# Last feed-forward down projection of a two-block model: seven block products instead of eight, in two parts of the contracted channels

## The reference, cut to what matters

```python
D_MODEL, D_FF = 1024, 2816
# block 2, after its mixers; x is (1, 1024 tokens, 1024 channels)
h = modulate(x, g_2, shift_2, scale_2)
u = depthwise_conv(h @ w_up_2, ffn_conv_w_2) + ffn_conv_b_2
gate, val = split(u, 2, axis=-1)
x = x + gate_2 * ((silu(gate) * val) @ w_down_2)      # 2816 -> 1024, the product of this case
out = rms_norm(x, final_norm_g_2)
```

## Time and profile before

| what | value |
|---|---|
| device time, median of 3 runs | 5803.57 us (5803.05 to 5805.03) |
| profiled execution: span of its instructions | 5800.0 us |
| mean granted TensorE clock | 0.923 of full speed |
| TensorE busy (matmuls) | 4973.6 us, 86% |
| VectorE, ScalarE, GpSimd busy | 1681.9, 1308.9, 551.3 us |
| last down projection, matmuls of L438 | 704, 305.1 us busy |
| the same, TensorE idle ahead of it | 16.7 us |

### The profile page before, as it was taken

One profiled execution on the slowest core, in us unless ns is written; L12 is line 12 of the kernel. 1 busy time (PEld: TensorE's weight loads), 2 busy tenths in 40 slices (PEclk: granted clock), 3 DMA queues, 4 the chain that ended last, 5 costly groups with the idle time before them and its releaser, 6 DMA issues. The chain is left out here.

```text
span 5800.0 us, 68474 instructions
## 1 busy us (share of the span) xinstructions
PE 4973.6 (86%) x27313; PEld 2658.2 (46%) x27313; DVE 1681.9 (29%) x3062; ACT 1308.9 (23%) x2074; POOL 551.3 (10%) x443
## 2 busy tenths in 40 slices
PE   6688888887989778999989778787888886999898
PEld 2254564532644533444434326556656632444344
DVE  5433243203611611111100145444515612111101
ACT  2222122102410611222200113222214402222100
POOL 0020121100010010000000013222200002000000
PEclk9898888898999889999999889888989998999999
DMA  3501101110021021111033111111010001111111
GB/s 76 81 18 33 31 7 34 34 44 11 1 74 47 33 87 33 36 40 36 29 113 107 42 39 38 43 43 40 7 39 1 1 29 33 40 36 40 31 40 52
DMA packets 301970, 232.18 MB, mean 40 GB/s; under 512 B 30771, under 2 KB 266982, under 8 KB 301670
## 3 DMA queue, kind: packets, MB, share of 16 engines
q1 hardware_dynamic: 301706, 228.40, 14.0%
HBM read 203.69 MB, written 24.67 MB: 39 GB/s over the span
## 5 line engine op out<-in xcount | busy, mean ns | idle before, releaser
L624 PE MATMUL psum<-ffn_in,up_slots 128*128 128x512 f32 x2816 | 1212.9, 594 | 54.3 <-DMA up_slots<-in_w_up_dram 35.8
L624 PEld LDWEIGHTS psum<-ffn_in,up_slots 128*128 128x128 f32 x2816 | 536.4, 191 | 730.8 <-issue 730.8
L661 DVE SCALAR_TENSOR_TENSOR conv<-u,conv_cols_a,conv 128x1024 f32<-128x1024 f32 x88 | 113.0, 1284 | 983.3 <-ACT conv L643 983.3
L438 PE MATMUL psum<-hidden,w_slots 128*128 128x512 f32 x704 | 305.1, 596 | 16.7 <-DMA w_slots<-in_w_down_dram 16.7
L2248 PE MATMUL psum<-hidden,w_slots 128*128 128x512 f32 x704 | 306.3, 596 | 9.6 <-DMA w_slots<-in_ffn_w_down_dram 9.6
L640 ACT ACTIVATE u<-psum 128x512 f32<-128x512 f32 x176 | 105.1, 597 | 892.8 <-PE psum L624 892.8
L2774 PE MATMUL psum<-h,w_slots 128*128 128x512 f32 (+1 forms) x576 | 219.7, 542 | 38.3 <-issue 36.1
L675 POOL TENSOR_TENSOR hidden<-conv 128x1024 f32 x44 | 103.1, 2343 | 1317.5 <-DVE conv L665 1317.5
L438 PEld LDWEIGHTS psum<-hidden,w_slots 128*128 128x128 f32 x704 | 134.7, 191 | 187.1 <-issue 169.6
L2248 PEld LDWEIGHTS psum<-hidden,w_slots 128*128 128x128 f32 x704 | 133.9, 191 | 176.7 <-issue 166.8
L1532 PE MATMUL psum<-x,w_slots 128*128 128x512 f32 x384 | 175.4, 620 | 34.1 <-issue 23.8
(11 more groups left out here) (552 smaller groups left out, 7504.7 us busy)
## 6 DMA issues: line engine op xcount, KB each, us to landing
mod_slots<-in_w_mod_dram SPq DMA_DIRECT2D x12, 2048.0 KB, 8.1
up_slots<-in_ffn_w_up_dram SPq DMA_DIRECT2D x44, 512.0 KB, 3.8
up_slots<-in_w_up_dram SPq DMA_DIRECT2D x44, 512.0 KB, 3.9
w_slots<-in_w_in_dram SPq DMA_DIRECT2D x38, 512.0 KB, 5.0
w_slots<-in_ffn_w_down_dram SPq DMA_DIRECT2D x8, 1408.0 KB, 12.4
w_slots<-in_w_down_dram SPq DMA_DIRECT2D x8, 1408.0 KB, 7.0
rows_in<-in_x_dram SPq DMA_DIRECT2D x16, 512.0 KB, 3.6
gate_w<-in_w_in_dram SPq DMA_DIRECT2D x16, 512.0 KB, 6.0
```

The costliest lines, as they stand in the source:

```text
L438: last = nc.tensor.matmul(T.ps[2 * s + j][:, :], slots[:, s, k, :], rhs(k)[:, j * HALF:(j + 1) * HALF], start=(k == 0), stop=(k == kt - 1))
L624: last = nc.tensor.matmul(T.ps[b][:, :], slots[:, q, k, :], h[:, k, j * HALF:(j + 1) * HALF], start=(k == 0), stop=(k == KD - 1))
L661: nc.vector.scalar_tensor_tensor(out=conv[:, q, :], in0=u[:, q, first:first + S], scalar=conv_w[first][:, bass.ds(col, 1)], in1=conv[:, q, :],
```

## The change

`block_product` takes the place of `add_product` in this one call. Output channels, contracted channels and tokens are each cut in two, and the four quarter results are made from seven products of quarter size instead of eight. A is the weight matrix: a11 and a12 are the weights of output block n (n = 0 to 3) from the first and second 11 blocks of contracted channels; a21 and a22 are those of output block n + 4. B is `hidden`: b11 and b12 are the first 11 channel blocks for the early and late 512 tokens, b21 and b22 the last 11.

The weight sums s1 = a21 + a22, s2 = s1 - a11, s3 = a11 - a21, s4 = a12 - s2 are made on GpSimd for each output pair. The activation sums t1 = b12 - b11, t2 = b22 - t1, t3 = b22 - b12, t4 = b21 - t2 are made on VectorE. t3 overwrites b12 in `hidden`, and s3 overwrites a21. The products are p1 = a11 b11, a12 b21, p6 = s2 t2, p7 = s3 t3, p5 = s1 t1, a22 t4 and s4 b22. With u2 = p1 + p6 and u3 = u2 + p7 the quarters are p1 + a12 b21, u2 + p5 + s4 b22, u3 + a22 t4 and u3 + p5.

The 11 blocks are handled in two parts, of 6 and then 5 blocks, so there are eight steps: (part 0, n = 0 to 3), then (part 1, n = 0 to 3). One step has seven products of 6 (or 5) matmuls of 512 columns. Step i uses banks 4 (i mod 2) to 4 (i mod 2) + 3. The turn between the parts, where VectorE remakes the t's for part 1, is in step 3 (`turn`). Four DMAs (384 KB each in part 0, 320 KB in part 1) load a step's weights.

```diff
--- before.py
+++ after.py
@@ -452,6 +452,161 @@
                                 nc.vector.scalar_tensor_tensor(
                                     out=xs, in0=T.ps[2 * s + j][:, :], scalar=gate[:, bass.ds(i * 2 + s, 1)],
                                     in1=xs, op0=ALU.mult, op1=ALU.add).then_inc(kept[2 * s + j], 1)
+def block_product(nc, T, w, rhs, x, gate):
+    KH = KF // 2
+    EARLY, LATE = slice(0, HALF), slice(HALF, S)
+    first_n = (KH + 1) // 2
+    spans = ((0, first_n), (first_n, KH))
+    pairs = KD // 2
+    steps = [(part, n) for part in range(2) for n in range(pairs)]
...
+    with sbuf(nc, "act_sums", [P, 3, first_n, HALF]) as act_sums, sbuf(nc, "down_slots", [P, 2, 2, 2, first_n, P]) as slots, \
+            sbuf(nc, "down_sums", [P, 2, 3, first_n, P]) as sums, sbuf(nc, "partial", [P, 2, HALF]) as partial, \
+            sbuf(nc, "partial_3", [P, HALF]) as partial_3:
...
+            weights = (weights_even, weights_odd)
+            width = lambda part: spans[part][1] - spans[part][0]
+            def weight(i, block_half, channel_half):
+                return slots[:, i % 2, block_half, channel_half, 0:width(steps[i][0]), :]
+            a11, a12, a21, a22 = (lambda i: weight(i, 0, 0)), (lambda i: weight(i, 0, 1)), (lambda i: weight(i, 1, 0)), (lambda i: weight(i, 1, 1))
+            s1, s2, s4 = (lambda i: sums[:, i % 2, 0, 0:width(steps[i][0]), :]), (lambda i: sums[:, i % 2, 1, 0:width(steps[i][0]), :]), \
+                (lambda i: sums[:, i % 2, 2, 0:width(steps[i][0]), :])
+            s3 = a21
+            b11 = lambda part: rhs[:, spans[part][0]:spans[part][1], EARLY]
+            b12 = lambda part: rhs[:, spans[part][0]:spans[part][1], LATE]
+            b21 = lambda part: rhs[:, KH + spans[part][0]:KH + spans[part][1], EARLY]
+            b22 = lambda part: rhs[:, KH + spans[part][0]:KH + spans[part][1], LATE]
+            t1, t2, t4 = (lambda part: act_sums[:, 0, 0:width(part), :]), (lambda part: act_sums[:, 1, 0:width(part), :]), \
+                (lambda part: act_sums[:, 2, 0:width(part), :])
+            t3 = b12
+            @block.sync
+            def _(sp):
+                for i, (part, n) in enumerate(steps):
+                    if i >= 2:
+                        sp.wait_ge(c12_made, i - 1)
+                    for bh in range(2):
+                        cols = weight_cols(w, KF, (n + bh * pairs) * P)
+                        for ch in range(2):
+                            sp.dma_start(weight(i, bh, ch), cols[:, ch * KH + spans[part][0]:ch * KH + spans[part][1], :]
+                                         ).then_inc(weights[i % 2], 16)
+            @block.gpsimd
+            def _(pool):
+                for i in range(len(steps)):
+                    pool.wait_ge(weights[i % 2], 64 * (i // 2 + 1))
+                    if i >= 2:
+                        pool.wait_ge(c12_made, i - 1)
+                    nc.gpsimd.tensor_tensor(s1(i), a21(i), a22(i), ALU.add).then_inc(sums_made, 1)
+                    pool.wait_ge(sums_made, 4 * i + 1)
+                    nc.gpsimd.tensor_tensor(s2(i), s1(i), a11(i), ALU.subtract).then_inc(sums_made, 1)
+                    nc.gpsimd.tensor_tensor(s3(i), a11(i), a21(i), ALU.subtract).then_inc(sums_made, 1)
+                    pool.wait_ge(sums_made, 4 * i + 2)
+                    nc.gpsimd.tensor_tensor(s4(i), a12(i), s2(i), ALU.subtract).then_inc(sums_made, 1)
+            @block.tensor
+            def _(pe):
+                def product(bank, lhs, moving, first=True):
+                    kt = lhs.shape[1]
+                    for k in range(kt):
+                        last = nc.tensor.matmul(T.ps[bank][:, :], lhs[:, k, :], moving[:, k, :], start=(first and k == 0), stop=(k == kt - 1),
+                                                skip_group_check=not first)
+                    return last
+                for i, (part, n) in enumerate(steps):
+                    ba, bb, bc, bd = (4 * (i % 2) + j for j in range(4))
+                    pe.wait_ge(weights[i % 2], 64 * (i // 2 + 1))
+                    if i >= 2:
+                        pe.wait_ge(c11_added, i - 1)
+                    product(ba, a11(i), b11(part)).then_inc(p1_made, 1)
+                    if n == 0:
+                        pe.wait_ge(acts_made, 4 * part + 4)
+                    pe.wait_ge(sums_made, 4 * i + 4)
+                    if i >= 2:
+                        pe.wait_ge(u2_made, i - 1)
+                    product(bb, s2(i), t2(part)).then_inc(p6_made, 1)
+                    pe.wait_ge(p1_kept, i + 1)
+                    product(ba, a12(i), b21(part), False).then_inc(c11_made, 1)
+                    if i >= 2:
+                        pe.wait_ge(c21_added, i - 1)
+                    product(bc, s3(i), t3(part)).then_inc(p7_made, 1)
+                    if i >= 2:
+                        pe.wait_ge(c12_added, i - 1)
+                    product(bd, s1(i), t1(part)).then_inc(p5_made, 1)
+                    pe.wait_ge(u3_made, i + 1)
+                    product(bc, a22(i), t4(part), False).then_inc(c21_made, 1)
+                    pe.wait_ge(c22_added, i + 1)
+                    product(bd, s4(i), b22(part), False).then_inc(c12_made, 1)
+            @block.scalar
+            def _(act):
+                for i in range(len(steps)):
+                    act.wait_ge(p1_made, i + 1)
+                    if i >= 2:
+                        act.wait_ge(u_added, 3 * (i - 1))
+                    nc.scalar.activation(partial[:, i % 2, :], T.ps[4 * (i % 2)][:, :], ACT.Copy).then_inc(p1_kept, 1)
+            @block.vector
+            def _(dve):
+                def add_to(out_block, tokens, src, added):
+                    xs = x[:, out_block, tokens]
+                    if gate is None:
+                        nc.vector.tensor_tensor(xs, xs, src, ALU.add).then_inc(added, 1)
+                    else:
+                        nc.vector.scalar_tensor_tensor(out=xs, in0=src, scalar=gate[:, out_block:out_block + 1], in1=xs,
+                                                       op0=ALU.mult, op1=ALU.add).then_inc(added, 1)
+                nc.vector.tensor_tensor(t1(0), b12(0), b11(0), ALU.subtract).then_inc(acts_made, 1)
+                dve.wait_ge(acts_made, 1)
+                nc.vector.tensor_tensor(t2(0), b22(0), t1(0), ALU.subtract).then_inc(acts_made, 1)
+                nc.vector.tensor_tensor(t3(0), b22(0), b12(0), ALU.subtract).then_inc(acts_made, 1)
+                dve.wait_ge(acts_made, 2)
+                nc.vector.tensor_tensor(t4(0), b21(0), t2(0), ALU.subtract).then_inc(acts_made, 1)
+                for i, (part, n) in enumerate(steps):
+                    ba, bb, bc, bd = (T.ps[4 * (i % 2) + j][:, :] for j in range(4))
+                    turn = part == 0 and n == pairs - 1
+                    u2 = partial[:, i % 2, :]
+                    dve.wait_ge(p6_made, i + 1)
+                    dve.wait_ge(p1_kept, i + 1)
+                    nc.vector.tensor_tensor(u2, u2, bb, ALU.add).then_inc(u2_made, 1)
+                    dve.wait_ge(c11_made, i + 1)
+                    add_to(n, EARLY, ba, c11_added)
+                    dve.wait_ge(p7_made, i + 1)
+                    dve.wait_ge(u2_made, i + 1)
+                    if i >= 1:
+                        dve.wait_ge(u_added, 3 * i)
+                    nc.vector.tensor_tensor(partial_3[:, :], u2, bc, ALU.add).then_inc(u3_made, 1)
+                    dve.wait_ge(p5_made, i + 1)
+                    add_to(n + pairs, LATE, bd, c22_added)
+                    if turn:
+                        nc.vector.tensor_tensor(t1(1), b12(1), b11(1), ALU.subtract).then_inc(acts_made, 1)
+                        dve.wait_ge(acts_made, 5)
+                        nc.vector.tensor_tensor(t2(1), b22(1), t1(1), ALU.subtract).then_inc(acts_made, 1)
+                        nc.vector.tensor_tensor(t3(1), b22(1), b12(1), ALU.subtract).then_inc(acts_made, 1)
+                    dve.wait_ge(u3_made, i + 1)
+                    dve.wait_ge(c22_added, i + 1)
+                    add_to(n + pairs, LATE, partial_3[:, :], u_added)
+                    dve.wait_ge(c21_made, i + 1)
+                    add_to(n + pairs, EARLY, bc, c21_added)
+                    if turn:
+                        dve.wait_ge(acts_made, 6)
+                        nc.vector.tensor_tensor(t4(1), b21(1), t2(1), ALU.subtract).then_inc(acts_made, 1)
+                    dve.wait_ge(c21_added, i + 1)
+                    add_to(n + pairs, EARLY, u2, u_added)
+                    add_to(n, LATE, u2, u_added)
+                    dve.wait_ge(c12_made, i + 1)
+                    dve.wait_ge(u_added, 3 * i + 3)
+                    add_to(n, LATE, bd, c12_added)
 
 
 def gated_merge(nc, T, w_gate, gate_col, bias, w_branch, h, o, merged):
@@ -3302,7 +3457,7 @@
             channel_rms(nc, T, x, h, KD, 0, S, gain, shift)
             conv_ffn_up(nc, T, A[up][0], conv_w, conv_b, h, hidden, lead)
         if mods is None:
```

(2 more changed lines are left out.)

4 lines of the change are left out of this document (added).

## The result

The changed kernel takes **5770.3 us** (median of 4 runs, 5767.25 to 5774.98) against 5803.31 us (4 runs, 5802.47 to 5805.03). The ratio is 0.9946, with a 95% interval from 0.9934 to 0.9958: 33.0 us faster, where 30.5 were forecast, inside the range of 5766.5 to 5780. The profiled execution took 5767.44 us with a span of 5765.7, 1.74 apart. The prediction's 3.57 for the kernel before is another thing, the distance from one profiled execution's span to the median of other executions, so that profiled execution was faster than the median one.

What follows compares the result with a forecast made beforehand. The prediction took TensorE to bound the stage. Its terms, -37.8 + 0.45 + 4.1 + 2.15 + 0.6, gave -30.5 us: span 5769.5, device time 5773 us, range 5766.5 to 5780.

Steps and rivals of the forecast that it cites:

- The bound: Last down projection: TensorE-bound, 88 matmuls fewer at an unchanged 0.4291 us each, -37.8 us.
- The second product's wait: First step: TensorE waits for s4 because VectorE's and GpSimd's sums collide, +4.1 us, bounds 0 and 7.7.
- turns of 0.64 us less each: Start of the stage: VectorE and GpSimd alternate, a pair of 1024-element additions costing 2.93 us against 3.57 alone.
- The clock: Behind the second product's idle stretch: TensorE falls to half clock for 4.3 us, +2.15 us, bounds 0 and 2.96.
- half clock in the first product: Start of the stage: TensorE starts at half clock, costing 2.96 us before and after, so no change.
- The later weights: Start of the stage: the first step's four DMAs carry 128 KB more, first matmul later by +0.45 us.
- The covers: Steady steps and joints between products: additions, evictions, copies, weight loads and sums all hidden, 0; joints' upper bound 1.5 us.
- the turn: Step 3, between the parts: VectorE remakes the t's in time, 0 with 0.8 us to spare, up to 1.5.
- The end: End of the stage: SyncE clears 19 semaphores instead of 10, +0.6 us.
- A: Start of the stage: the sums don't collide, so no idle stretch or second clock fall, 5767 us; chance 0.16.
- B: Start, turn and joints: more of the new dependence shows as stalls, 5780 us; chance 0.15, including values between.
- C: Joints between products: small gaps keep TensorE's clock low, making the kernel slower, 5903 us; chance 0.04.

Runs made afterwards that it cites:

- two queues: Changed kernel with half of the first two steps' weights issued by ScalarE's queue instead of SyncE's: stage 283.49 us against 283.47.
- sums in turn: Changed kernel with GpSimd's first sum held until VectorE has made t4: stage 285.43 us against 283.47.
- finer waits: Changed kernel with each product waiting only for the sums it reads: stage 278.54 us against 283.47, median 5761.39 us, ratio 0.9934 to the kernel before.
- early first product: Changed kernel with products reordered, each awaiting only its own sums, the first starting once its 384 KB landed: stage 273.77 us against 283.47, median 5761.03 us.
- the first experiment: Changed kernel without VectorE's four activation sums of part 0, so its output differs: stage 277.50 us against 283.47.

## Why the prediction was right

- **The bound.** TensorE was the limit of the stage, and 88 matmuls fewer at an unchanged pace are 37.8 us. The eighth product, put back, cost as much once the clock's share is taken out.
- **The second product's wait** was seen in its place, with its cause and nearly its size (4.1 against 4.48). Without VectorE's sums it vanished, and with the engines kept apart it stayed. So the mechanism holds, with one correction: the price is the sum of both engines' work, and not their meeting. By turns of 0.64 us less each, from rows 9, the second product was to start 19.84 us into the stage; it started at 20.27. The sums of 3072 elements took 3.36 where 3.3 had been reckoned, which is 0.2 of the difference. The Trainium skill's page SBUF — State Buffer (Terms, shared port pair) has the loser blocked for the whole of the other's instruction, which had given 20.84. The changed kernel agrees in kind, and its 20.27 lies between the two reckonings; kept apart the engines needed 20.83.
- **The clock** fell as forecast, at 1.49 us for 2.15. Within one kernel the size repeats: 1.49 and 1.48 us in the two traces of the changed kernel. Between kernels it does not follow the idle time: 1.52 us behind 3.65 us of it (two queues), 3.09 behind 4.25 (eighth product), 2.88 behind 5.21 (sums in turn). What sets it was not found, so one other place could not be relied on for it, and that it came within 0.7 is luck. My bounds of 0 to 2.96 were too narrow at the top by 0.1. With 1.01 us of idle time (finer waits) it did not fall. The half clock in the first product, which I had left as it was, cost 1.8 us (two queues) to 3.0 us (early first product).
- **The later weights** were mis-sized, +0.45 for +1.08. The step that went wrong is the one that gave the first four loads the whole bandwidth and added only their 128 KB. By the windows shown with the two queues, 0.46 MB beyond the first product's own weights had moved before it started, against 0.29 before, and 0.17 MB at 290 GB/s are the missing 0.6 us. (The second trace of before began 6.87 us after the issue and not 7.17, so the term itself is known to 0.3.) It cost nothing, since it lies beside the wait for the sums: a further 1.27 us changed the stage by 0.02. The table's +1.08, -0.57 and +4.48 are thus one term, the second product at 20.27 us instead of the 7.17 + 5.15 + 2.96 = 15.28 of a kernel without sums: +4.99, where I had 4.55.
- **The sum.** Its terms were off by +0.6, -0.6, +0.4, -0.7 and -0.1 us, in the table's order, and these nearly cancel: 30.8 for 30.5. That it is so close is luck, while the device time's 33.0 and 29.3 us in two comparisons show how far a median of four or five runs can be trusted. The range did not need the luck. The 0.66 us behind the stage were in no term.
- **The covers held.** None of the 54 later products waits; the turn had 1.26 us to spare, for 0.8 forecast. The end cost 0.48 for 0.6.
- **The rivals.** A (no meeting, 5767 us) is refuted by the first experiment and by the 4.96 and 4.80 us of the held sums, though single runs of the changed kernel were as low as 5766.16. B's stalls at the turn and between the products did not appear. C did not happen: PEclk was 1.00 over the 252 us from 5492 to 5744, in groups of 12 and 10 matmuls. The Trainium skill's account of a bf16 kernel whose clock goes back and forth as it cycles through banks (TensorE: Matmul & The Clock Gate, A second HAM failure mode) has no counterpart in this stage; its one fall came behind an idle stretch of over 4 us.

```profile
5492.00:5744.00 252.00, 249.98 (x583) 110.51 (x581) 62.42 (x75) 4.18 (x7) 38.50 (x24) 1.00 0.12 34
```

(The window of rival C's test, of the changed kernel.)
